# First condition by halves of the channels, x squared on ScalarE, and the later conditions moved into the v and u strips

## The reference

```python
cond = silu(c) @ ada_w + ada_b
shift1, scale1, gate1, shift2, scale2, gate2 = jnp.split(cond, 6, axis=-1)
h = modulate(rmsnorm(x, norm1_g), shift1, scale1)
z = h @ w_in + b_in
u, v, val, gate = jnp.split(z, [512, 1024, 1536], axis=-1)
y_a = spatial_gating_mixer(gelu(u), gelu(v), ...)
y_b = conformer_conv_mixer(val, gate, ...)
y = concatenate([rmsnorm(y_a, g_a), rmsnorm(y_b, g_b)], axis=-1)
x = x + gate1 * (y @ w_out)
```

## Time and profile before

| what | us |
|---|---|
| runs (3): median | 791.32 |
| runs: lowest to highest | 785.7 to 792.75 |
| profiled execution | 789.66 |
| its span in the profile | 787.9 |

### The profile page before, as it was taken

One profiled execution on the slowest core, in us unless ns is written; L12 is line 12 of the kernel. 1 busy time (PEld: TensorE's weight loads), 2 busy tenths in 40 slices (PEclk: granted clock), 3 DMA queues, 4 the chain that ended last, 5 costly groups with the idle time before them and its releaser, 6 DMA issues.

```text
span 787.9 us, 13085 instructions
## 1 busy us (share of the span) xinstructions
PE 719.9 (91%) x5423; PEld 563.0 (71%) x5424; DVE 366.7 (47%) x745; ACT 326.4 (41%) x696; POOL 60.8 (8%) x71
## 2 busy tenths in 40 slices
PE   6798999889999999999999999997999998778785
PEld 4385678787999999999988777785865554344352
DVE  1452998554755444555478679544441111011011
ACT  2243485363743333454448896668421111001001
POOL 5000002000000000100000009062000000000000
PEclk9899899889999999999999999999999999899899
DMA  8997856633966656553554436355999999999994
GB/s 317 406 372 286 304 219 268 237 107 109 370 215 215 214 179 215 202 182 135 178 187 148 157 108 222 107 214 213 343 393 422 419 422 420 422 420 421 418 406 142
DMA packets 71476, 211.44 MB, mean 268 GB/s; under 512 B 7352, under 2 KB 34134, under 8 KB 55543
## 3 DMA queue, kind: packets, MB, share of 16 engines
q1 hardware_dynamic: 70370, 209.91, 70.3%
q0 software_dynamic: 800, 0.63, 0.5%
q10 hardware_dynamic: 244, 0.03, 0.0%
HBM read 209.51 MB, written 1.05 MB: 267 GB/s over the span
## 4 chain that ended last, share of the span: by engine, by line
PE 67%; DMA 15%; DVE 7%; ACT 6%; issue 3%; SPq 2%; ACTq 0%; DVEq 0%
PE ps L1906 10%; PE ps L1907 9%; PE ps L1908 9%; DMA ring<-in_expert_w_gate_dram 7%; PE ps L1919 5%; PE ps L2590 5%; PE ps L1920 5%; PE ps L1921 5%; DMA ring<-in_expert_w_up_dram 4%; PE ps L1988 3%; DMA ring<-in_ada_w_dram 2%; SPq L431 2%; DVE ring_low L1177 2%; PE ps L2632 2%; PE ps L2561 2%
## 5 line engine op out<-in xcount | busy, mean ns | idle before, releaser
L1177 DVE TENSOR_TENSOR ring_low<-ring,HI 128x1024 fp32r<-128x1024 f32 (+1 forms) x119 | 142.3, 1237 | 45.9 <-ACT HI L667 45.8
L667 ACT ACTIVATE HI<-ring 128x1024 fp32r<-128x1024 f32 (+1 forms) x135 | 133.9, 1056 | 42.4 <-DMA ring<-in_w_in_dram 41.4
L1906 PE MATMUL ps<-AH,HI 128*128 128x256 f32 x320 | 90.1, 282 | 0.3 <-DVE Z L1423 0.3
L1908 PE MATMUL ps<-AH,ring_low 128*128 128x256 f32 x320 | 89.6, 280 | 0.0
L1907 PE MATMUL ps<-AL,HI 128*128 128x256 f32 x320 | 89.5, 280 | 0.0
L2590 PE MATMUL ps<-ring,ZM 128*32 128x256 f32 x880 | 73.6, 422 | 16.1 <-DMA ring<-in_expert_w_up_dram 11.2
L1906 PE MATMUL ps<-HI,AH 128*128 128x512 f32 (+1 forms) x176 | 71.6, 407 | 2.1 <-DVE ring_low L1177 1.0
L1907 PE MATMUL ps<-ring_low,AH 128*128 128x512 f32 (+1 forms) x176 | 68.9, 392 | 0.0
L1908 PE MATMUL ps<-HI,AL 128*128 128x512 f32 (+1 forms) x176 | 68.5, 389 | 0.0
L2590 PEld LDWEIGHTS ps<-ring,ZM 128*32 128x32 f32 x880 | 35.1, 121 | 44.0 <-DMA ring<-in_expert_w_up_dram 14.1
L1906 PEld LDWEIGHTS ps<-AH,HI 128*128 128x128 f32 x320 | 60.1, 188 | 3.1 <-issue 2.5
(11 more groups left out here) (381 smaller groups left out, 1325.8 us busy)
## 6 DMA issues: line engine op xcount, KB each, us to landing
ring<-in_expert_w_up_dram SPq DMA_DIRECT2D x28, 1024.0 KB, 26.3
ring<-in_expert_w_gate_dram SPq DMA_DIRECT2D x27, 1024.0 KB, 26.4
ring<-in_ada_w_dram SPq DMA_DIRECT2D x24, 1024.0 KB, 8.6
ring<-in_expert_w_down_dram SPq DMA_DIRECT2D x23, 1024.0 KB, 23.8
ring<-in_w_ffn_in_dram SPq DMA_DIRECT2D x20, 1024.0 KB, 6.1
ring<-in_w_in_dram SPq DMA_DIRECT2D x17, 1024.0 KB, 5.7
ring<-in_w_ffn_out_dram SPq DMA_DIRECT2D x11, 1024.0 KB, 7.1
ring<-in_w_out_dram SPq DMA_DIRECT2D x8, 1024.0 KB, 4.9
```

The costliest lines, as they stand in the source:

```text
L667: act(HI[:, i % UNITS, 0:w], W.view(name)[:, o:o + w], ACT.Copy).then_inc(s_hi, 1)
L1177: tt(W.low(name)[:, o:o + w], W.view(name)[:, o:o + w], HI[:, i % UNITS, 0:w].bitcast(F32), ALU.subtract).then_inc(s_lo, 1)
L1906: mm(dst, lh, rh, start=start, stop=False)
L1908: return mm(dst, ll, rh, start=False, stop=stop)
```

## The change

The ring loads of quarter 0 are now `ada_half`: each holds 256 rows of 512 shift and 512 scale columns, two pieces in one slot. Four of them give shift and scale of channels 0 to 511, four those of the rest. `columns_half` turns a half with eight matmuls of two columns. Value and gate go by halves of the channels too: in_v0, in_g0 (operand tiles 0 to 3), then in_v1, in_g1 (tiles 4 to 7); the second half of quarter 0 is multiplied in between. ScalarE squares x itself, with the sum over the row, in place of four squares, 16 sums on TensorE and a root of them. GpSimd waits for the fourth half load to be used before it issues its small loads. Quarter 1 goes into the v strip (1, 2, 2 and 3 steps behind the four units), its columns behind the first u unit; quarter 2 into the u strip (0, 2, 3 and 3 steps). VectorE copies quarter 1 behind the norm of v. SyncE's new order is in the diff. Left out below are renumbered semaphore counts.

```diff
@@ -101,13 +101,13 @@
 def split_order():
-    out = ["in_v0", "in_v1", "in_v2"] + [f"{w}{h}" for w in ("in_g", "in_u", "in_w", "kv_v") for h in "01"]
+    out = [f"{w}{h}" for h in "01" for w in ("in_v", "in_g")] + [f"{w}{h}" for w in ("in_u", "in_w", "kv_v") for h in "01"]
     out += [f"out{h}" for h in range(4)] + ["fx0", "fy0"]
...
     out += [f"{w}{h}" for w in ("q", "k", "v", "u", "pool", "attn", "wq", "wo") for h in "01"]
-    width = {"kw": 8 * (NZ - 2560), "in_v0": 1024, "in_v2": 1024, "kv_k0": 1024, "kv_k2": 1024}
+    width = {"kw": 8 * (NZ - 2560), "kv_k0": 1024, "kv_k2": 1024}
     return [(n, width.get(n, 2048)) for n in out]
@@ -240,7 +241,7 @@
         rows1, rows2, rowsc = rows[:, 0:P], rows[:, P:2 * P], rows[:, 2 * P:3 * P]
-        SQA = tiles(Zf[:, 2048:4096], 8)
+        SQA = tiles(Zf[:, 2048:4096], 2)
         XR, SQX = YT[:, :, :], YT[:, :, :]
@@ -446,6 +447,14 @@
+            def ada_half(h, ks):
+                for k in ks:
+                    load(f"ada0{4 * h + k}", (s_ada, 4 * h + k + 1), *(
+                        (lambda v, i=i: v[:, 1024 * i:1024 * i + 1024].rearrange("p (s n) -> p s n", s=2),
+                         A["ada_w"][:, 0:2048].rearrange("(p k) (s n) -> p k s n", p=P, s=2)[:, 2 * k + i, :, 512 * h:512 * h + 512])
+                        for i in range(2)))
@@ -456,33 +465,30 @@
             const(X[:, :, :], A["x"].rearrange("o (t p) d -> p (o t) d", p=P), s_x)
-            ada(A["ada_w"], 0, range(7), 0)
-            rows128("in_v0", w_in, 1024, 512, 0, 2)
-            ada(A["ada_w"], 0, (7,), 0)
-            rows128("in_v1", w_in, 1024, 512, 2, 4)
-            rows128("in_v2", w_in, 1024, 512, 6, 2)
-            ada(A["ada_w"], 1, (0, 1), 2048)
+            ada_half(0, range(4))
+            rows128("in_v0", w_in, 1024, 512, 0, 4)
+            ada_half(1, (0,))
+            rows128("in_g0", w_in, 1536, 512, 0, 4)
+            ada_half(1, (1, 2, 3))
+            rows128("in_v1", w_in, 1024, 512, 4, 4)
+            rows128("in_g1", w_in, 1536, 512, 4, 4)
             const(wsv, A["a_spatial_w"].rearrange("o h t s -> t (o h) s"), s_ws)
-            rows128("in_g0", w_in, 1536, 512, 0, 4)
-            ada(A["ada_w"], 1, (2, 3), 2048)
-            rows128("in_g1", w_in, 1536, 512, 4, 4)
-            ada(A["ada_w"], 1, (4, 5), 2048)
             load("brow_v", (s_un, S.first["in_u0"] + 1), (lambda s: s[0:1, 0:512], A["b_in"][:, 512:1024]))
             rows128("in_u0", w_in, 512, 512, 0, 4)
-            ada(A["ada_w"], 1, (6, 7), 2048)
+            ada(A["ada_w"], 1, (0, 1, 2), 2048)
             rows128("in_u1", w_in, 512, 512, 4, 4)
-            ada(A["ada_w"], 2, (0, 1), 4096)
...
                 const(MX[t], A["mem_2"].rearrange("o (t p) d -> p (o t) d", p=P)[:, t, :], s_mem)
+            ada(A["ada_w"], 1, (3, 4, 5, 6, 7), 2048)
             rows128("in_w0", w_in, 0, 512, 0, 4)
-            ada(A["ada_w"], 2, (2, 3), 4096)
+            ada(A["ada_w"], 2, (0, 1), 4096)
             rows128("in_w1", w_in, 0, 512, 4, 4)
-            ada(A["ada_w"], 2, (4, 5), 4096)
             rows128("kv_v0", w_kv, 512, 512, 0, 4)
-            ada(A["ada_w"], 2, (6, 7), 4096)
+            ada(A["ada_w"], 2, (2, 3, 4), 4096)
             rows128("kv_v1", w_kv, 512, 512, 4, 4)
+            ada(A["ada_w"], 2, (5, 6, 7), 4096)
             for h in range(4):
@@ -592,6 +598,8 @@
+            po.wait_ge(s_ada, 4)
@@ -712,29 +720,34 @@
-            for kk in range(4):
-                ac.wait_ge(s_xc, kk + 1)
-                act(SQA[:, 2 * kk:2 * kk + 2, :], XC[:, 2 * kk:2 * kk + 2, :], ACT.Square).then_inc(s_sqs, 1)
             warm(ACT.Sqrt)
-            rooted(RTS[0], ps[4][:, 0:2], SUM_X)
-            hi_to(0)
-            ac.wait_ge(s_m, 1)
-            for k in range(8):
-                if k % 2 == 0:
-                    ac.wait_ge(s_xc, 4 + k // 2 + 1)
-                act(AH[:, k, :], XR[:, k, :], ACT.Identity, scale=colm[:, 0, k:k + 1], bias=colv[:, 0, k:k + 1]).then_inc(s_ah, 1)
-                if k in (1, 4):
-                    hi_to(1 + k // 4)
-            for u in range(4):
-                hi_to(u + AHEAD)
+            ac.wait_ge(s_x, 16)
+            for t in range(NT):
+                act(SQA[:, t, :], X[:, t, :], ACT.Square, accum_out=RTS[0][:, t:t + 1]).then_inc(s_sqs, 1)
+            ac.wait_ge(s_sqs, SQ_X + 2)
+            act(RTS[0], RTS[0], ACT.Sqrt, scale=1.0 / D, bias=eps[:, 0:1]).then_inc(s_rn, 1)
+            def upper_half(h):
+                hi_to(4 * h)
+                ac.wait_ge(s_m, h + 1)
+                for k in range(4 * h, 4 * h + 4):
+                    if k % 2 == 0:
+                        ac.wait_ge(s_xc, 4 + k // 2 + 1)
+                    act(AH[:, k, :], XR[:, k, :], ACT.Identity, scale=colm[:, 0, k:k + 1], bias=colv[:, 0, k:k + 1]).then_inc(s_ah, 1)
+                    if k % 4 == 1:
+                        hi_to(4 * h + 1)
+            upper_half(0)
+            hi_to(3)
+            upper_half(1)
+            hi_to(7)
...
                     ACT.Copy).then_inc(s_wt, 1)
-            for u in range(4, 8):
-                hi_to(u + AHEAD)
+            hi_to(S.first["in_u0"] + 1)
@@ -1223,38 +1235,53 @@
                 copy(XC[:, 2 * kk:2 * kk + 2, :], tiles(ps[kk][:, :], 2)).then_inc(s_xc, 1)
-            ve.wait_ge(s_rp, 1)
-            copy(C1[:, 0:ROWS1], ps[5][:, 0:ROWS1]).then_inc(s_rc, 1)
             recip(RTS[0], SUM_X)
...
                    ALU.mult).then_inc(s_xc, 1)
-            lo_to(0)
-            condition(1, 7)
-            columns(1, 7, C1[:, B0:B0 + 16])
-            scales(0, colv[:, 0, 8:16], C1[:, N1:N1 + 8], 1)
-            ve.wait_ge(s_m, 1)
-            ve.wait_ge(s_xc, 8)
-            for k in range(9):
-                if k < 8:
-                    ts(HTM[:, k, :], XR[:, k, :], colm[:, 0, k:k + 1], colv[:, 0, k:k + 1], ALU.mult, ALU.add).then_inc(s_xc, 1)
-                if k:
-                    ve.wait_ge(s_xc, 8 + k)
-                    ve.wait_ge(s_ah, OP_X + k)
-                    tt(AL[:, k - 1, :], HTM[:, k - 1, :], AH[:, k - 1, :].bitcast(F32), ALU.subtract).then_inc(s_al, 1)
-                if k in (2, 5):
-                    lo_to(1 + k // 4)
-            for u in range(4):
-                lo_to(u + AHEAD)
+            ve.wait_ge(s_rp, 1)
+            copy(C1[:, 0:ROWS1], ps[5][:, 0:ROWS1]).then_inc(s_rc, 1)
+            def half(c):
+                return c.rearrange("p (s h b) -> p s h b", s=2, h=2)
+            def lower_half(h):
+                ve.wait_ge(s_ada, 4 * h + 4)
+                if h:
+                    ve.wait_ge(s_cnp, 1)
+                copy(CN[:, 0, :], ps[7][:, :]).then_inc(s_cn, 1)
+                ve.wait_ge(s_cnp, h + 1)
+                ve.wait_ge(s_rc, 1)
+                tt(half(colv[:, 0, :])[:, :, h, :], ps[7][:, 0:8].rearrange("p (b s) -> p s b", b=4),
+                   half(C1[:, B0:B0 + 16])[:, :, h, :], ALU.add).then_inc(s_col, 1)
+                ve.wait_ge(s_col, h + 1)
+                stt(colm[:, 0, 4 * h:4 * h + 4], colv[:, 0, 8 + 4 * h:12 + 4 * h], 1.0, C1[:, N1 + 4 * h:N1 + 4 * h + 4], ALU.add,
+                    ALU.mult).then_inc(s_m, 1)
+                ve.wait_ge(s_m, h + 1)
+                ve.wait_ge(s_xc, 8)
+                for k in range(4 * h, 4 * h + 5):
+                    if k < 4 * h + 4:
+                        ts(HTM[:, k, :], XR[:, k, :], colm[:, 0, k:k + 1], colv[:, 0, k:k + 1], ALU.mult, ALU.add).then_inc(s_xc, 1)
+                    if k > 4 * h:
+                        ve.wait_ge(s_xc, 8 + k)
+                        ve.wait_ge(s_ah, OP_X + k)
+                        tt(AL[:, k - 1, :], HTM[:, k - 1, :], AH[:, k - 1, :].bitcast(F32), ALU.subtract).then_inc(s_al, 1)
+                    if k % 4 in (1, 3):
+                        lo_to(4 * h + k % 4 // 2)
+            lower_half(0)
+            lo_to(3)
+            lower_half(1)
+            lo_to(7)
...
             copy(cw[:, :, 0:TAPS], ps[6][:, 0:4 * TAPS].rearrange("p (j c) -> p c j", c=4)).then_inc(s_rc, 1)
-            for u in range(4, 8):
-                lo_to(u + AHEAD)
-            condition(2, 7)
+            lo_to(S.first["in_u0"] + 1)
@@ -1262,7 +1289,6 @@
             ve.wait_ge(s_rc, 3)
-            columns(2, 7, C2[:, B1:B1 + 16])
@@ -1277,8 +1303,9 @@
             iu, iw = S.first["in_u0"], S.first["in_w0"]
+            taps(0, 2)
             lo_to(iu + AHEAD)
-            taps(0, 4)
+            taps(2, 4)
@@ -1311,8 +1338,11 @@
                    ALU.mult).then_inc(s_tn, 1)
+            condition(2, 7)
+            taps(18, 20)
+            columns(2, 7, C2[:, B1:B1 + 16])
             lo_to(iw + 1 + AHEAD)
-            taps(18, 22)
+            taps(20, 22)
             lo_to(iw + 2 + AHEAD)
@@ -1989,9 +2019,27 @@
+            def ada_half(h, kp):
+                name = f"ada0{4 * h + kp}"
+                te.wait_ge(*W.ready(name))
+                for j in range(4):
```

(62 more changed lines are left out.)

27 lines of the change are left out of this document (13 added, 14 removed).

## The result

The changed kernel takes 808.0 us (median of 4 runs, 804.13 to 811.59) beside 792.04 for the kernel before (4 runs, 785.7 to 796.99) on the same chip: ratio 1.019, 95% interval 1.014 to 1.024. It is slower by 16 us, and 807 was forecast. The profiled execution took 804.13, with a span of 802.2.

A forecast was written before the change was run, and what follows sets the result against it. TensorE is busy 91% of the span, and loads in_w0 and in_w1 pace the stretch. Strip 15 us earlier, in_w1 22 later relative to it, then 51 instead of 41.4 to the sums: 17 late, 807 us, range 790 to 819.

The forecast's parts named there:

- Front: Start to first split matmul: half the first condition's bytes are needed, so that matmul comes at 26.5 instead of 37.33.
- Strip: Start of the v strip on TensorE: taken as 66, 15 us before the old 80.76; terms summed to 68.
- in_w0: Load in the v strip: issued at V + 7.7 behind ada1 5 to 7, landing at 84; TensorE idles 7 us.
- V: The time at which the v strip starts on TensorE, from which the prediction counts later steps; taken as 66.
- Fourth v unit: In the v strip: five diagonals and this unit take about 10 us after the idle time, ending at V + 33.
- in_w1: Load behind ada2 1, whose slot the fourth v unit frees: lands at V + 40 = 106, 7 us later than before.
- VectorE's waits: VectorE, nearly full before, now waits about 13 us for in_w0, 9 for in_w1 and 8 for MH.
- The root of y_a behind out0: Behind the sums over y_a: out0's copy delays this root about 3 us, beside the third kv_v unit.
- the 6.99 us of sums: TensorE's sums over x's squares in the front: their removal was claimed not to end on the path.
- Rival A: In_w0 and in_w1 land before ScalarE asks, so the strip's 15 us arrive: 778, faster; chance 0.11.
- Rival C: TensorE's clock: every new idle stretch is followed by the low level, plus 26 us: 816; chance 0.12.
- Rival B: Only the in_w0 part holds; in_w1 lands at 99.5 and the early strip pays for late loads: 790; chance 0.15.

The follow-up runs named there:

- the version with places and order: The changed kernel with quarter 1's first steps back among value and gate units, its copy and columns earlier, and SyncE's order rewritten to suit: 780.69 us, again 779.23.
- a new order: The changed kernel with only SyncE's order of ring loads behind in_g1 rewritten, the work on every engine unchanged: 796.2 us, ratio 1.005 to the kernel before.
- new places: The changed kernel with only the condition steps on TensorE and VectorE's copy and columns moved earlier, SyncE's order kept: 802.96 us, ratio 1.012 to the kernel before.
- the best version with the sums: The version with places and order, but x's squares summed by TensorE again, in 16 sums: 785.91 us, ratio 0.990 to the kernel before.

## Why the prediction was right

The mechanism and nearly every step hold. By its own terms:

- **Front.** The fourth half load was to land at 17.4: its step starts at 17.09. `columns_half` was to take 3.5 at the low clock: 3.58. The second time it took 1.95, where 2.85 was forecast. First split matmul 26.5: it came at 25.35, mostly because the load's matmuls took 1.06, not 1.9.
- **Strip.** 66 between bounds of 63.5 and 72: 65.85. The prediction's own sum gave 68, and no term takes the 2 us off; from the first split matmul on, its 41.5 were 40.5. That the choice of 66 met the trace is luck.
- **in_w0.** Issue at V + 7.7 = 73.7: 75.47. The first v unit took 4.5 us (65.85 to 70.39) and not 2.9: the granted clock was 0.50 in 67 to 69, and the prediction had this unit at the full clock. From issue to landing 10.15: 8.9. The two errors have opposite signs, so the landing at 84.36, where 84 was forecast, is in part luck. The idle time 7: 6.33.
- **Fourth v unit.** V + 33 = 99: 96.82. Its five diagonals took the 4.49 of the low clock, but the unit itself was back at the full clock and took 3.2 instead of about 5. This term was 2 us too large. The forecast at the sums is too late by as much (157 against 155.19), though by the terms only 1.1 of it had reached in_w1's landing (106 against 104.87) and 0.7 arose behind it.
- **in_w1.** 7.3 us from issue to landing: 7.65. From there to the end of the norm of v 11.9: 11.9 (104.87 to 116.75). To the end of the fourth u unit 36.8: 36.5. ada2 7 on an otherwise empty queue 4.6: 4.53. The Trainium skill's page "DMA: Bandwidth & Descriptors" (section "Anatomy of one DMA — SWDGE (gpsimd) path") gives an estimate of 4.4 by a fit taken on DMAs that GpSimd issues; this one is issued by SyncE, and the trace's 4.53 comes near it. TensorE's wait for it 2.6: 2.75. The sums at in_w1 + 51: + 50.3.
- **VectorE's waits.** 13, 9 and 8: 12.71, 7.39 and 8.69.
- **The root of y_a behind out0.** "Beside the third kv_v unit", at no cost: this was wrong. TensorE waits 2.09 for it at 162.87. It doesn't show in the sum, since the next mark, the first sums of 128x1 over the channels of y, is 14.2 us later than before (197.98 against 183.80), less than the 15.0 at y_a.

Two readings of the old kernel do not hold. The low clock in 78 to 87 was put down to an idle time of 3.17 ahead of it. But the changed kernel has the same fall at the start of its v strip, behind the four bias matmuls of one row, with TensorE busy in all of 62.9 to 69; and a wait of 2.75 was followed once by the full clock and once, at 2.74, by the low one. What decides it is not shown here.

The other is the one on the squares: the 6.99 us of sums were taken to be off the path in the old kernel. Alone they were worth 4.7 us at the sums and 1.2% of the time (0.5 to 1.8%). It did not spoil the forecast, since the front was worked out from its first load anew and not by subtraction; but a forecast of that part alone would have been wrong.

Rival A, "the loads do not decide", was priced at 778, and the version with places and order was measured at 779 to 781. Its price is about right, but not by its mechanism: it wanted in_w0 by 71 and in_w1 by 84, and in that version their high parts start at 77.37 and 91.90, the second after a wait of 8.20, with the v strip at 70.24 and not at 66. What kept the changed kernel from this time is shown: order and places together. Rival C, the clock, shows in the rows (0.52 and 0.57 behind the idle times); behind these two it was worth 2.5 us at most. The low level elsewhere (the first v unit 1.6 us, the columns of the front 1.6) no run took away on purpose. Rival B did not occur, since in_w1 came at 104.87 and not at 99.5.

## What to carry to other kernels

Read a queue that issues in order as part of the path: list for each load the slot that it takes, the instruction that frees the slot, and what stands behind it in the queue. A work step that frees slots is not free to move, since it carries later loads with it: here a new order gave back 8.5 us, new places 3.7, and the two worked out together 22.8. A load moved up in the queue also hands its slot to another load, as in_w0 did to ada2 2. And when a wait is removed, look at the next one on the same chain before counting the gain.

## What the runs showed of the hardware

- A 128x512 matmul in float32 took 0.88 us at a granted clock of 1.00, in two records of 0.44 (11.43 us for 26 records); the split matmuls of the same shape come every 0.23 us. I had expected 0.5 for it.
- Matmuls of one and of two columns cost the same for each record: 16 records of two columns took 3.58 us at a granted clock of 0.50, and 1.95 to 1.98 at 0.95 to 1.00, and 32 records of one column 6.99 and 3.73, which is 0.22 and 0.12 for each.
- The same 32 records of the sums took 6.99 us in one kernel and 3.73 in another, at a granted clock that reads 1.00 in both stretches. So at the start of a program that column does not tell the speed, and the records' own durations (0.352 and 0.250 us) have to be read; why they differ is open. (The first is the kernel before, the second the best version with the sums.)
- The clock in the front differs from one execution to the next. Ten profiled executions have the new front without the sums: in nine the first columns took 3.35 to 3.58, in one, whose only change lies 60 us later, 1.95. With the sums in front they took 1.98, and one execution can't tell whether the sums did it.
- The granted clock also fell while TensorE was busy: in the changed kernel it was 1.00 in 62.9 to 66.4 and 0.50 in 67 to 69, behind four matmuls of one row, without an idle time between. The first v unit took 4.5 us instead of 2.9 in all seven traces that have its steps where the change put them.
